# Second block of a two-block mixer kernel: a new order of the chunk inverse, half of the output projection multiplied ahead, three down tiles ahead, and the store by tiles

## The reference, cut to what matters

```python
xn = rms_norm(h, pre_mix_norm);  proj = xn @ w_in
y_ssd  = ssd_mixer(...)                        # 512 channels
y_rwkv = rwkv7_mixer(...)                      # 512 channels, 8 heads of 64
    # S = S * w_t + (S @ a_t) b_t + v_t k_t;  y_t = S @ r_t     (state 64 x 64, per head)
    # y = (y - mean) * rsqrt(var + 64e-5) * ln_w + ln_b         (per head)
    # y = (y + bonus) * g
mix = concat([y_ssd, y_rwkv]) @ w_out          # 1024 x 1024
h = h + rms_norm(mix, post_mix_norm)
hn = rms_norm(h, pre_ffn_norm)
u = causal_dwconv(hn @ ffn_w_up);  gate, val = split(u)         # 1024 x 5632
h = h + rms_norm((silu(gate) * val) @ ffn_w_down, post_ffn_norm) # 2816 x 1024
```

## Time and profile before

| what | us |
|---|---|
| median of three runs | 1747.25 (1745.02 to 1748.61) |
| profiled execution, its own time | 1746.78 |
| its span | 1745.0 |
| PE busy (matmul) | 1576.2, 90% |
| the scan (L2232 to L2441), 1164.7 to 1280.3 | 115.6 |
| its norm, to 1299.2 | 18.9 |
| output projection, to 1366.4 | 67.2 |
| up, to 1609.6 | 243.2 |
| down, last matmul about 1731.2 | 121.6 |
| from there to the end | 13.8 |

### The profile page before, as it was taken

How to read it: one execution, slowest core, us unless ns; L and a number is a source line. 1 busy time by engine, 2 the same in 40 slices (tenths; PEclk the granted TensorE clock), 3 DMA queues, 4 the chain that set the end, 5 groups by cost and what they waited for, 6 DMA issues and landing times. The chain is left out here.

```text
span 1745.0 us, 30548 instructions
## 1 busy us (share of the span) xinstructions
PE 1576.2 (90%) x12917; PEld 1347.0 (77%) x12917; DVE 760.3 (44%) x1238; ACT 676.7 (39%) x1091; POOL 446.7 (26%) x114
## 2 busy tenths in 40 slices
PE   3899999979969999998989999878959999997996
PEld 3788888767757878997879887658948888886885
DVE  3401014759986521127854434485464333333002
ACT  3311121138874421127744543541233455554111
POOL 1422322200013233220023342107033244444341
PEclk9899999989989999999999999988979999998998
DMA  8444321036502022136121331000021222222221
GB/s 331 149 183 156 146 71 64 1 81 146 110 27 73 1 103 91 49 137 153 44 97 62 132 106 47 1 2 4 28 73 49 97 97 96 96 96 73 95 97 48
DMA packets 31241, 153.19 MB, mean 88 GB/s; under 512 B 6664, under 2 KB 8200, under 8 KB 16656
## 3 DMA queue, kind: packets, MB, share of 16 engines
q1 hardware_dynamic: 29808, 150.62, 25.9%
q10 hardware_dynamic: 1312, 0.80, 0.2%
HBM read 129.39 MB, written 2.10 MB: 75 GB/s over the span
## 5 line engine op out<-in xcount | busy, mean ns | idle before, releaser
L215 PE MATMUL banks<-even_token_parts,even_weight_parts 128*128 128x512 f32 (+1 forms) x1296 | 235.8, 342 | 0.0
L215 PE MATMUL banks<-ffn_token_parts,ffu_weight_parts 128*128 128x512 f32 (+1 forms) x1056 | 231.2, 381 | 2.6 <-POOL ffu_weight_parts L196 2.3
L215 PEld LDWEIGHTS banks<-ffn_token_parts,ffu_weight_parts 128*128 128x128 f32 x1056 | 192.8, 189 | 40.7 <-POOL ffu_weight_parts L196 2.5
L215 PEld LDWEIGHTS banks<-even_token_parts,even_weight_parts 128*128 128x128 f32 x1296 | 198.3, 188 | 32.6 <-issue 2.9
L196 POOL TENSOR_TENSOR out_half<-weight_chunk,out_half 128x2048 fp32r<-128x2048 f32 x12 | 57.2, 4788 | 391.1 <-ACT out_half L190 386.8
L196 POOL TENSOR_TENSOR ffu_weight_parts<-weight_chunk,ffu_weight_parts 128x2048 fp32r<-128x2048 f32 x22 | 101.6, 4619 | 170.2 <-ACT ffu_weight_parts L190 170.2
L196 POOL TENSOR_TENSOR even_weight_parts<-weight_chunk,even_weight_parts 128x2048 fp32r<-128x2048 f32 x16 | 73.7, 4608 | 226.9 <-ACT even_weight_parts L190 226.9
L2649 PE MATMUL banks<-ffd_weight_parts,ffn_f_parts 128*128 128x512 f32 x528 | 121.6, 393 | 9.7 <-PEq L2533 9.7
L2649 PEld LDWEIGHTS banks<-ffd_weight_parts,ffn_f_parts 128*128 128x128 f32 x528 | 100.2, 190 | 31.1 <-issue 10.1
L215 PE MATMUL banks<-sec_token_parts,sec_weight_parts 128*128 128x512 f32 (+1 forms) x528 | 115.5, 376 | 0.3 <-PEq L268 0.3
L2602 DVE SCALAR_TENSOR_TENSOR ffn_conv<-banks,b_ffn_taps,ffn_conv 128x511 f32<-128x511 f32 (+1 forms) x88 | 61.9, 745 | 114.6 <-ACT ffn_conv L2576 111.5
(11 more groups left out here) (424 smaller groups left out, 2868.5 us busy)
## 6 DMA issues: line engine op xcount, KB each, us to landing
weight_chunk<-in_ffn_up SPq DMA_DIRECT2D x22, 1024.0 KB, 4.8
weight_chunk<-in_w_in_even SPq DMA_DIRECT2D x16, 1024.0 KB, 6.8
even_pT<-in_w_mod SPq DMA_DIRECT2D x16, 1024.0 KB, 4.9
weight_chunk<-in_w_in SPq DMA_DIRECT2D x13, 1024.0 KB, 4.8
weight_chunk<-in_w_out SPq DMA_DIRECT2D x12, 1024.0 KB, 4.8
weight_chunk<-in_w_in_odd SPq DMA_DIRECT2D x12, 1024.0 KB, 4.7
weight_chunk<-in_ffn_down SPq DMA_DIRECT2D x11, 1024.0 KB, 4.8
front_w<-in_w_mod SPq DMA_DIRECT2D x8, 1024.0 KB, 12.5
```

The costliest lines, as they stand in the source:

```text
L215: m = self.nc.tensor.matmul(o, w, env.tok[:, tp, k, a:b], start=n == 0, stop=n == 3 * KD - 1)
```

## The change

- **Inverse.** POOL cuts nothing. `one` multiplies N itself with X, and DVE applies the level's mask to the result on its way to `t1` (L2642 of the new code). `two` makes only the update of X. Both run over the four quarters of the array (`TILES4`). X transposed is no longer kept: PE transposes X anew each level (`flip`, 8 transposes per half), and ACT copies it out. The additions of the unit matrix stand between the masks.
- **Projection ahead.** The first half of the depth (`y_ssd`, features 0 to 511) is split in the scan's last part (ACT, POOL), and its product with one half of the columns, 48 of the 192 matmuls, stands in the norm's block (`ahead_tile`). The order of the column chunks of `w_out` is turned for that. `stage_out_rest` does the other 144 and the same tail as before, all eight banks in use, no bank shared by tiles.
- **Norm.** `ln_w * g` and `bonus + ln_b` are made by ACT at the scan's end; DVE multiplies y with the first, and the bonus term with g, before the variance is known; behind it stand 16 multiplications of 128 x 128 and 4 additions.
- **Seam.** Three of the four tiles of the first down chunk (`EARLY_DOWN`, 36 matmuls, banks 4 to 7, 0 and 1) stand at the end of the up block.
- **End and store.** The last two down chunks are done tile by tile, the last tile by halves of its columns; each tile is stored when it is ready, the last in two halves.

```diff
+def mixed_lo(env, mixed, i):
+    hi = mixed_part(env, 0, i).bitcast(F32)
+    return env.nc.gpsimd.tensor_tensor(mixed_part(env, 1, i), mixed[:, :, i * P : (i + 1) * P], hi, ALU.subtract)
...
+def ahead_tile(env, wide, i):
+    for k in range(FT):
+for n, (wp, tp) in enumerate(PASSES):
+    m = env.nc.tensor.matmul(
+        bank(env, 2 * i + 1), env.tok[:, tp, k, i * P : (i + 1) * P], wide[0][:, wp, k, :], start=k == 0 and n == 0, stop=False)
+    return m
...
+def stage_out_rest(env, x, gate, gain, mix, ring, wide, next_ring, junk):
...
+def _(pool):
+    pool.wait_ge(mix_lo, TX)
+    for c in range(2, ring.chunks):
+        ring.lo(pool, c, c % 2)
+    for s in range(2):
+        next_ring.lo(pool, s, s)
...
+    for i in range(TX):
+        pe.wait_ge(mix_lo, i + 1)
+        for k in range(FT, KD):
+            for n, (wp, tp) in enumerate(PASSES):
+                m = nc.tensor.matmul(
+                    bank(env, 2 * i + 1), env.tok[:, tp, k, cols(i)], wide[0][:, wp, k, :], start=False, stop=k == KD - 1 and n == 2)
+        m.then_inc(product, 1)
+    pe.wait_ge(ring.lo_done, ring.chunks)
+    for i in range(TX):
+        for k in range(KD):
+            if i >= 2 and k == 2:
+                turn(i - 2)
+            for n, (wp, tp) in enumerate(PASSES):
+                m = nc.tensor.matmul(
+                    bank(env, 2 * i), env.tok[:, tp, k, cols(i)], wide[1][:, wp, k, :], start=k == 0 and n == 0, stop=k == KD - 1 and n == 2)
+        m.then_inc(product, 1)
...
-        def blocks(b, at, stationary, moving):
+        def one(b, lv):
+            pe.wait_ge(x_out[b], lv)
             for a in range(2 * FT):
-                for c, h in DIAGONAL:
+                for c, h in TILES4:
+                    at = (4 * b + c) * BANK + a * HD
                     m = nc.tensor.matmul(
-                        env.PS[half(c), (at + h) * BANK + a * HD : (at + h) * BANK + (a + 1) * HD],
-                        stationary[half(c), col(2 * a + h)], moving[half(c), col(2 * a + h)], start=True, stop=True)
-            return m
-        def one(b, lv):
-            pe.wait_ge(cut[b], lv + 1)
-            pe.wait_ge(x_out[b], lv)
-            blocks(b, 4 * b, nT(b, lv), home(G_X, b)).then_inc(first[b], 1)
+                        env.PS[half(h), at : at + HD], home(G_N, b)[half(c), col(2 * a + h)], home(G_X, b)[half(c), col(2 * a + h)],
+                        start=True, stop=True)
+            m.then_inc(first[b], 1)
         def two(b, lv):
             pe.wait_ge(t1_out[b], lv)
             pe.wait_ge(xt_out[b], lv)
-            if lv < LEVELS - 1:
-                blocks(b, 4 * b, xt(b), t1(b)).then_inc(second[b], 1)
-            blocks(b, 4 * b + 2, t1(b), xt(b)).then_inc(third[b], 1)
+            for a in range(2 * FT):
+                for c, h in TILES4:
+                    at = (4 * b + h) * BANK + a * HD
+                    m = nc.tensor.matmul(
+                        env.PS[half(c), at : at + HD], turned(b)[half(h), a, c, :], cuts(b)[half(h), c, a, :], start=True, stop=True)
+            m.then_inc(second[b], 1)
+        def flip(b, lv):
+            pe.wait_ge(x_out[b], lv + 1)
+            for a in range(2 * FT):
+                at = (4 * b + 2) * BANK + a * P
+                m = nc.tensor.transpose(env.PS[:, at : at + P], home(G_X, b)[:, a * P : (a + 1) * P], env.ident[:])
+            m.then_inc(flipped[b], 1)
+        for b in range(2):
+            pe.wait_ge(masked, PAIRS - 1 + b)
+            one(b, 1)
+            flip(b, 0)
         for lv in range(1, LEVELS):
             for b in range(2):
-                one(b, lv)
+                two(b, lv)
             for b in range(2):
-                two(b, lv)
+                if lv < LEVELS - 1:
+                    one(b, lv + 1)
+                flip(b, lv)
...
+        for i in LATER_TILES:
+            pool.wait_ge(mixed_hi, i - LATER_TILES[0] + 1)
+            mixed_lo(env, mixed, i)
...
-        for lv in range(1, LEVELS):
+        for lv in range(LEVELS - 1):
             for b in range(2):
-                act.wait_ge(first[b], lv)
-                if lv >= 2:
-                    act.wait_ge(third[b], lv - 1)
-                nc.scalar.copy(pairs(t1(b)), by_head(4 * b)).then_inc(t1_out[b], 1)
+                act.wait_ge(flipped[b], lv + 1)
+                nc.scalar.copy(xt(b), two_banks(4 * b + 2)).then_inc(xt_out[b], 1)
+        for b in range(2):
+            act.wait_ge(flipped[b], LEVELS)
+            done(nc.scalar.copy, b, 0)
...
-        dve.wait_ge(masked, PAIRS)
-        for b in range(2):
-            nc.vector.tensor_tensor(tiles(home(G_X, b)), tiles(home(G_X, b)), eye(16), ALU.add).then_inc(x_out[b], 1)
-            dve.wait_ge(cut[b], 1)
-            nc.vector.tensor_tensor(tiles(xt(b)), tiles(nT(b, 0)), eye(16), ALU.add).then_inc(xt_out[b], 1)
+            if p in (4, PAIRS - 1):
+                b = p // 4 - (p == 4)
+                dve.wait_ge(masked, 4 * (b + 1))
+                nc.vector.tensor_tensor(tiles(home(G_X, b)), tiles(home(G_X, b)), eye(16), ALU.add).then_inc(x_out[b], 1)
         for lv in range(1, LEVELS):
             for b in range(2):
-                if lv < LEVELS - 1:
-                    dve.wait_ge(second[b], lv)
-                    dve.wait_ge(x_out[b], lv)
-                    x = pairs(home(G_X, b))
-                    nc.vector.tensor_tensor(x, by_head(4 * b), x, ALU.add).then_inc(x_out[b], 1)
-                dve.wait_ge(third[b], lv)
-                dve.wait_ge(xt_out[b], lv)
-                nc.vector.tensor_tensor(pairs(xt(b)), by_head(4 * b + 2), pairs(xt(b)), ALU.add).then_inc(xt_out[b], 1)
+                dve.wait_ge(first[b], lv)
+                nc.vector.tensor_tensor(
+                    tiles(t1(b)), tiles(two_banks(4 * b)), C2["level"][:, lv, :].unsqueeze(1).to_broadcast([P, 16, HD]), ALU.mult).then_inc(t1_out[b], 1)
+            for b in range(2):
+                dve.wait_ge(second[b], lv)
+                dve.wait_ge(x_out[b], lv)
+                x = pairs(home(G_X, b))
+                nc.vector.tensor_tensor(x, by_head(4 * b), x, ALU.add).then_inc(x_out[b], 1)
+        for b in range(2):
+            dve.wait_ge(flipped[b], LEVELS)
+            done(nc.vector.tensor_copy, b, 1)
...
+        ahead_tile(env, wide, LATER_TILES[0])
         pe.wait_ge(inverse_ready, 1)
         for f in range(FT):
-            head_spread(env, 4, var, f).then_inc(spread_ready, 1)
+            for j in range(TX):
+                rows = slice(32 * j, 32 * (j + 1))
+                m = nc.tensor.matmul(bank(env, 2 * j, P, f * P), C2["spread"][rows, f, :], var[rows, :], start=True, stop=True)
+        m.then_inc(spread_ready, 1)
+        for i in LATER_TILES[1:]:
+            ahead_tile(env, wide, i)
+        for i in range(LATER_TILES[0]):
+            pe.wait_ge(mixed_done, i + 1)
+            ahead_tile(env, wide, i)
...
+            v = pT[:, T_V + f, :]
+            nc.vector.tensor_tensor(v, v, W["g"][:, f, :], ALU.mult).then_inc(shifted, 1)
+        def weight(f):
+            dve.wait_ge(centred, f + 1)
+            dve.wait_ge(squared, f + 1)
+            nc.vector.tensor_tensor(y[:, f, :], y[:, f, :], gained(G)[:, f, :], ALU.mult).then_inc(weighted, 1)
+        weight(0)
+        weight(1)
         dve.wait_ge(sums_ready, 1)
-        nc.vector.tensor_scalar(var[:], bank(env, 4, P), 1.0 / HD, RWKV_GN_EPS, ALU.mult, ALU.add).then_inc(var_ready, 1)
+        nc.vector.tensor_scalar(var[:], bank(env, 0, P), 1.0 / HD, RWKV_GN_EPS, ALU.mult, ALU.add).then_inc(var_ready, 1)
+        weight(2)
         dve.wait_ge(root_ready, 1)
         nc.vector.reciprocal(var[:], var[:]).then_inc(inverse_ready, 1)
-        dve.wait_ge(centred, FT)
-        dve.wait_ge(spread_ready, FT)
+        weight(3)
+        dve.wait_ge(spread_ready, 1)
         for f in range(FT):
-            nc.vector.scalar_tensor_tensor(
-                by_tile(y[:, f, :]), by_tile(y[:, f, :]), C2["ln_w"][:, f : f + 1], spread_view(env, 4, f), ALU.mult, ALU.mult).then_inc(normed, 1)
+            dve.wait_ge(weighted, f + 1)
+            for j in range(TX):
+                tile = y[:, f, j * P : (j + 1) * P]
+                nc.vector.tensor_tensor(tile, tile, bank(env, 2 * j, P, f * P), ALU.mult).then_inc(normed, 1)
+        dve.wait_ge(shifted, FT)
         for f in range(FT):
-            dve.wait_ge(normed, f + 1)
-            nc.vector.scalar_tensor_tensor(
-                y[:, f, :], y[:, f, :], C2["ln_b"][:, f : f + 1], pT[:, T_V + f, :], ALU.add, ALU.add).then_inc(shifted, 1)
-        for f in range(FT):
-            dve.wait_ge(shifted, f + 1)
-            nc.vector.tensor_tensor(y[:, f, :], y[:, f, :], W["g"][:, f, :], ALU.mult)
+            dve.wait_ge(normed, TX * (f + 1))
+            nc.vector.tensor_tensor(y[:, f, :], y[:, f, :], pT[:, T_V + f, :], ALU.add)
...
+        for s in range(2):
+            ring.hi(act, 1, s)
...
+        pe.wait_ge(down_ring.lo_done, 1)
+        pe.wait_ge(lo_done, 2 + 2)
```

(31 more changed lines are left out.)

285 lines of the change are left out of this document (222 added, 63 removed).

## The result

| | median us | runs | against the kernel before, 95% interval |
|---|---|---|---|
| before | 1747.65 | 4 (1745.02 to 1748.61) | |
| changed | 1707.64 | 4 (1706.38 to 1708.57) | 0.9771 [0.9757, 0.9786] |
| changed, again in a later comparison | 1704.41 | 5 (1703.76 to 1705.75) | 0.9751 [0.9738, 0.9764] |

What follows compares the result with a forecast made beforehand. PE was taken to bound the inverse, with PE waiting at the seam and end. From 1746.8 us, -24.0 + 1.2 - 8.2 - 9.5 - 6.6 = -47.1 gave 1699.7, called 1700; range 1693 to 1712.

Steps and rivals of the forecast that it cites:

- The inverse, -24.0: Inverse: matmuls on four array quarters and no wait for POOL's cuts bring `solve` to 1215.8 instead of 1239.8, -24.0 us.
- a level is 6.8: Inverse: one level takes 6.8 us instead of 11.2, a 6.4 cycle plus four changes of array division at 0.1.
- third rival: Inverse: a floor of 25 ns for each record makes a call 1.6, a level 8.6, the total 1709.5 us; 3%.
- The scan's rest: Scan behind the inverse: ACT's ten more copies and POOL's two low parts cost nothing, no change.
- The norm, +1.2: Norm block: DVE ends within 0.5 us of before, but PE's 48 matmuls now end the block, +1.2 us.
- The projection, -8.2: Output projection: with 48 matmuls already done, its window takes 59.0 us instead of 67.2, -8.2.
- The wait of 2.7 for `lo(1)`: Output projection: PE waits 2.7 us ahead of the up projection, since `lo(1)` on DVE stands behind `residual(2)`.
- The loss to a lower clock that I had at the block's start: Output projection: PE idles 2 us at the block's start, and a lower clock behind it costs 0.9 us.
- The seam, -9.5: Between up and down: 36 early down matmuls fill 8.2 of 9.8 us in which PE idled, -9.5 us.
- The end, -6.6: Behind the last matmul: a shorter chain and a 256 KB last store landing in 2.6 give 7.2 instead of 13.8, -6.6 us.
- Ahead of the scan, 0: Stages ahead of the scan: no change in time, 0 us.
- slowest rival: Inverse: four quarters overlap no more than two, at 1.2 GHz; level 16.9, inverse loses 37 us, total 1761; 1%.

Runs made afterwards that it cites:

- doubled `one`: The changed kernel with every call of `one` from level 2 on issued twice, the same products into the same place: 1720.87 us.
- DVE order: The changed kernel with affine(1) ahead of the third tile's residual product, lo(1) ahead of its addition, and tile 2's transposition on PE 12 matmuls later: 1700.84 us.

## Why the prediction was right, and where not

- **The inverse, -24.0: the step that failed.** It was -18.4, in the later profiles up to -19.8. `one(0)` came at 1180.76 in a profile that was 3.3 us late by then, so 1.1 ahead of the forecast; the clock was 1.00; a call took 1.09, a flip 1.03 with its joint. Hops and changes of the array's division were as counted: less the delay of the stops the four levels are 7.1, 6.7, 6.7 and 6.7 us. The term that was mis-sized is "a level is 6.8". It took 8.2 on average: 5.6 us over four. (The 1.1 that the start was ahead went again: 0.3 up to the first `two`, 0.7 behind the last, with a stop of 0.64 in it.) The working had counted what a record costs in the array (14 ns) and never what it costs to bring it there (30 ns). The doubled `one` and the packets show that this is the bound.
- The third rival, the floor of 25 ns a record of the Trainium skill ("TensorE: Matmul & The Clock Gate", Wait — 56ns, not 53.3ns?), had the right form for another reason. Its level of 8.6 and its total of 1709.5 are nearer to what was measured than the forecast's. But the array does start a matmul each 14 ns; the floor is about 30 ns, a mean over 128 and more, and stands in the supply.
- **The scan's rest**: -1.1, part of it the clock, which differs between runs (39.7 to 40.9). Nothing of the added copies shows.
- **The norm, +1.2**: from its first matmul 18.5 became 20.7, +2.1. PE ended the block, as the prediction has it, 2.6 us behind DVE, whose sixteen small multiplications took 3.25 where I had 4.3. Moving one tile across the end of the block gives 2.5 back, in this stage and the next together.
- **The projection, -8.2**: -8.7. The wait of 2.7 for `lo(1)` was found at its place with 2.59. The loss to a lower clock that I had at the block's start came behind this wait. The DVE order shows both.
- **The seam, -9.5**: -10.0 with the down product's faster start; idle 1.58 against the forecast's 1.6.
- **The end, -6.6**: -7.1; the half store took 2.0, not 2.6.
- **Ahead of the scan, 0**: +3.3. "Nothing is edited" is not "nothing moves": behind the same 1.99 us of idling the stage had a lower clock for more or less of its length, from kernel to kernel. In the later run of the changed kernel, which had 44.6 us from the low-rank matmuls to the scan where the first had 46.4, the total is 4.4 above the forecast.
- **The total inside its range** is in part the range's width. It had 3 us for a slower inverse, where 5.6 were missing, and none for the stages ahead, where 3.3 were lost; the room that the projection, the seam and the end left unused took the rest.
- **Sums of the working that do not come out.** Rows 2 give 29.2 ns a record for a level of 11.2 us, not 29.5. The slowest rival's loss of 37 us does not follow from its level of 16.9: four such levels are 40 us more than four of 6.8 and the ends some 8 to 13 more, so the inverse would lose 24 to 29 and the total be 1748 to 1753, not 1761.
